# End of a decoder kernel: root table loaded at the down projection, decode tokens over four partition groups, first residual tile ahead of the last tile

## The reference

```python
hp = rms_norm(y_p, g_ffn_pre[l])
hs = rms_norm(y_s, g_ffn_pre[l])
y_p = y_p + rms_norm(swiglu(hp, w_gate[l], w_up[l], w_down[l]), g_ffn_post[l])
y_s = y_s + rms_norm(swiglu(hs, w_gate[l], w_up[l], w_down[l]), g_ffn_post[l])
```

## Time and profile before

| | |
|---|---|
| time before, median of 3 runs | 991.49 us (990.19 to 991.56) |
| the profiled execution | 988.71 us; span from first to last instruction 986.50 |
| granted TensorE clock, mean | 0.985 |
| PE busy | 942.6 us, 96% |
| DVE, ACT, POOL busy | 443.1, 356.3, 170.9 us |
| DMA | 105.85 MB, 107 GB/s over the span |

### The profile page before, as it was taken

One profiled execution on the slowest core, in us unless ns is written; L12 is line 12 of the kernel. 1 busy time (PEld: TensorE's weight loads), 2 busy tenths in 40 slices (PEclk: granted clock), 3 DMA queues, 4 the chain that ended last, 5 costly groups with the idle time before them and its releaser, 6 DMA issues.

```text
span 986.5 us, 18130 instructions
## 1 busy us (share of the span) xinstructions
PE 942.6 (96%) x7734; PEld 876.2 (89%) x7734; DVE 443.1 (45%) x900; ACT 356.3 (36%) x565; POOL 170.9 (17%) x46
## 2 busy tenths in 40 slices
PE   3999999899899999999899999999999999999997
PEld 2999998776699999976379999999999999999996
DVE  5799975765354677111453572222222222001103
ACT  5442224574454463135334543222222222222111
POOL 3000000000000001300030003433333333353330
PEclk9999999889999999999899989999999999999999
DMA  7304205342251358358051101222222232222202
GB/s 213 109 34 130 87 2 199 123 130 87 86 171 54 124 171 295 132 213 341 1 171 44 43 28 60 85 85 85 87 91 94 96 100 75 86 76 75 86 33 91
DMA packets 85343, 105.85 MB, mean 107 GB/s; under 512 B 9473, under 2 KB 72834, under 8 KB 85154
## 3 DMA queue, kind: packets, MB, share of 16 engines
q1 hardware_dynamic: 85056, 104.92, 32.0%
q10 hardware_dynamic: 226, 0.05, 0.0%
HBM read 98.26 MB, written 6.70 MB: 106 GB/s over the span
## 4 chain that ended last, share of the span: by engine, by line
PE 86%; DVE 8%; ACT 3%; issue 2%; DMA 1%; ACTq 0%; DVEq 0%
PE pall L1796 55%; PE pall L1808 7%; PE pall L2130 5%; PE pall L1833 4%; PE pall L2177 2%; PE pall L1820 2%; PE pall L2188 1%; PE pall L1886 1%; PE pall L1986 1%; DVE a_s L1434 1%; PE pall L1869 1%; PE pall L1890 1%; PE pall L2224 1%; PE pall L1995 1%; PE pall L1852 1%
## 5 line engine op out<-in xcount | busy, mean ns | idle before, releaser
L627 POOL TENSOR_TENSOR w_lo<-w_raw,w_hi 128x2048 fp32r<-128x2048 f32 (+1 forms) x36 | 161.2, 4476 | 622.8 <-ACT w_hi L670 332.1
L1796 PE MATMUL pall<-x_hi,w_hi 128*128 128x272 f32 x1024 | 213.5, 290 | 0.0
L1796 PE MATMUL pall<-x_lo,w_hi 128*128 128x272 f32 x1024 | 212.0, 288 | 0.0
L1796 PE MATMUL pall<-x_hi,w_lo 128*128 128x272 f32 x1024 | 210.6, 287 | 0.0
L1796 PEld LDWEIGHTS pall<-x_lo,w_hi 128*128 128x128 f32 x1024 | 161.5, 189 | 0.0
L1796 PEld LDWEIGHTS pall<-x_hi,w_hi 128*128 128x128 f32 x1024 | 160.5, 189 | 0.8
L1796 PEld LDWEIGHTS pall<-x_hi,w_lo 128*128 128x128 f32 x1024 | 160.6, 189 | 0.0
L670 ACT ACTIVATE w_hi<-w_raw 128x2048 fp32r<-128x2048 f32 (+1 forms) x61 | 114.7, 1880 | 91.4 <-PE pall L1796 91.4
L1796 PE MATMUL pall<-g_hi,w_hi 128*128 128x272 f32 x352 | 73.1, 289 | 0.0
L1796 PE MATMUL pall<-g_lo,w_hi 128*128 128x272 f32 x352 | 72.7, 288 | 0.0
L1796 PE MATMUL pall<-g_hi,w_lo 128*128 128x272 f32 x352 | 72.6, 287 | 0.0
(11 more groups left out here) (387 smaller groups left out, 1639.7 us busy)
## 6 DMA issues: line engine op xcount, KB each, us to landing
w_raw<-in_w_gate SPq DMA_DIRECT2D x10, 1024.0 KB, 5.3
w_raw<-in_w_up SPq DMA_DIRECT2D x10, 1024.0 KB, 5.3
w_raw<-in_w_in SPq DMA_DIRECT2D x8, 1024.0 KB, 6.5
w_raw<-in_w_down SPq DMA_DIRECT2D x8, 1024.0 KB, 4.9
dm_kv<-in_cache_mem_v SPq DMA_DIRECT2D x5, 1024.0 KB, 13.9
w_raw<-in_w_out SPq DMA_DIRECT2D x4, 1024.0 KB, 6.1
d_k<-in_cache_k SPq DMA_DIRECT2D x16, 256.0 KB, 3.0
d_v<-in_cache_v SPq DMA_DIRECT2D x16, 256.0 KB, 4.2
```

The costliest lines, as they stand in the source:

```text
L627: e.tensor_tensor(w_lo[:, n % 2, 0:w], w_raw[:, n % 2, 0:w], w_hi[:, n % 2, 0:w].bitcast(F32), ALU.subtract)\
L1796: ins = mm(acc(j)[:, a, :], w, x[:, k_x + k, a * HALF:(a + 1) * HALF], start=first and k == 0 and s_, stop=last and k == kts - 1 and t_)
```

## The change

Five edits, all at the end of the kernel:

1. ACT takes a root that nobody reads before the fourth unit of the down projection (n = `U_DOWN + 3`).
2. The decode tokens' part of `zg` tile k goes to partitions 32(k % 4) to 32(k % 4) + 31, columns 128(k // 4) onwards, of `y_tok[:, 4, :]`, so that the tile is 128 x 256 and not 32 x 1024. The same holds for the decode tile of the residual. Both use a matmul with the identity instead of a transpose. The decode sum is taken four times, once for each group of 32 partitions.
3. One root and one reciprocal of 128 x 5 replace two of each.
4. `y_transposes(0)` moves into `zg_transposes`, between the last two tiles (k = 6 and 7).
5. `y_sample` is stored in four transfers, one for each group of partitions, each row of which holds two pieces of 128 columns.

```diff
+                for q in range(4):
+                    store(O["y_sample"].rearrange("b t (j q c) -> q (b t) j c", j=2, q=4)[q],
+                          y_tok[32 * q:32 * q + 32, t, 0:256].rearrange("p (j c) -> p j c", j=2))
...
+            if n == U_DOWN + 3:
+                e.activation(small[:, 60:61], small[:, EPS_COL:EPS_COL + 1], ACT.Sqrt)
...
-        e.activation(small[:, Y_RSTD:Y_RSTD + 4], bank(4)[:, 0:4], ACT.Sqrt, bias=small[:, EPS_COL:EPS_COL + 1]).then_inc(S("norm_root"), 1)
-        e.activation(small[0:NS_TOK, Y_RSTD + 4:Y_RSTD + 5], bank(4)[0:NS_TOK, 4:5], ACT.Sqrt,
-                     bias=small[0:NS_TOK, EPS_COL:EPS_COL + 1]).then_inc(S("norm_root"), 1)
+        e.activation(small[:, Y_RSTD:Y_RSTD + 5], bank(4)[:, 0:5], ACT.Sqrt, bias=small[:, EPS_COL:EPS_COL + 1]).then_inc(S("norm_root"), 1)
...
-                e.tensor_copy(y_tok[0:NS_TOK, 4, k * P:(k + 1) * P], bank(b + 1)[0:NS_TOK, 0:P]).then_inc(S("zgT_out"), 1)
+                rows = slice(32 * (k % 4), 32 * (k % 4) + 32)
+                e.tensor_copy(y_tok[rows, 4, k // 4 * P:(k // 4 + 1) * P], bank(b + 1)[rows, 0:P]).then_inc(S("zgT_out"), 1)
...
+            cols = D if t < 4 else 256
             e.wait_ge(S("yT_full"), t + 1)
+            e.scalar_tensor_tensor(out=y_tok[:, t, 0:cols], in0=y_tok[:, t, 0:cols], scalar=small[:, Y_RSTD + t:Y_RSTD + t + 1],
+                                   in1=y_banks(t)[:, 0:cols], op0=ALU.mult, op1=ALU.add).then_inc(S("y_ready"), 1)
...
+        def y_transposes(t):
+            for k in range(KT):
+                if t < 4:
+                    ins = e.transpose(y_banks(t)[:, k * P:(k + 1) * P], yT[:, k, t * P:(t + 1) * P], ident[:])
+                else:
+                    rows = slice(32 * (k % 4), 32 * (k % 4) + 32)
+                    ins = mm(y_banks(t)[rows, k // 4 * P:(k // 4 + 1) * P], yT[:, k, NP_TOK:TOK], ident[:], start=True, stop=True)
+            ins.then_inc(S("yT_full"), 1)
...
-                e.transpose(bank(b + 1)[0:NS_TOK, 0:P], zg[:, k % 2, NP_TOK:TOK], ident[:]).then_inc(S("zgT_full"), 1)
+                mm(bank(b + 1)[32 * (k % 4):32 * (k % 4) + 32, 0:P], zg[:, k % 2, NP_TOK:TOK], ident[:], start=True, stop=True).then_inc(S("zgT_full"), 1)
+                if k == KT - 2:
+                    y_transposes(0)
...
-        y_transposes(0)
-
         e.wait_ge(*counted("n5", "add", KT - 1))
         e.wait_ge(S("zgT_out"), 2 * KT - 2)
-        for t in range(5):
-            w = P if t < 4 else NS_TOK
-            ins = mm(bank(4)[0:w, t:t + 1], sqacc[:, t * P:t * P + w], ones[:, 0:1], start=True, stop=True)
+        for t in range(4):
+            mm(bank(4)[:, t:t + 1], sqacc[:, t * P:(t + 1) * P], ones[:, 0:1], start=True, stop=True)
+        for q in range(4):
+            ins = mm(bank(4)[32 * q:32 * q + 32, 4:5], sqacc[:, NP_TOK:TOK], ones[:, 0:1], start=True, stop=True)
         ins.then_inc(S("norm_sum"), 1)
-        e.wait_ge(acc_out, J_DOWN + KT)
         y_transposes(1)
```

More of the change, by code:

```diff
@@ L610, in _ @@
             else:
-                store(O["y_sample"].rearrange("b t d -> (b t) d"), y_tok[0:NS_TOK, t, :])
+                for q in range(4):
+                    store(O["y_sample"].rearrange("b t (j q c) -> q (b t) j c", j=2, q=4)[q],
+                          y_tok[32 * q:32 * q + 32, t, 0:256].rearrange("p (j c) -> p j c", j=2))
         e.wait_ge(S("k_stored0"), 48)
@@ L1760, in _ @@
                 e.tensor_copy(y_tok[:, 0:4, k * P:(k + 1) * P], bank(b).rearrange("p (t c) -> p t c", t=4)).then_inc(S("zgT_out"), 1)
-                e.tensor_copy(y_tok[0:NS_TOK, 4, k * P:(k + 1) * P], bank(b + 1)[0:NS_TOK, 0:P]).then_inc(S("zgT_out"), 1)
-        e.wait_ge(*counted("n5", "root", 2))
-        e.reciprocal(small[:, Y_RSTD:Y_RSTD + 4], small[:, Y_RSTD:Y_RSTD + 4])
-        done(e.reciprocal(small[0:NS_TOK, Y_RSTD + 4:Y_RSTD + 5], small[0:NS_TOK, Y_RSTD + 4:Y_RSTD + 5]))
+                rows = slice(32 * (k % 4), 32 * (k % 4) + 32)
+                e.tensor_copy(y_tok[rows, 4, k // 4 * P:(k // 4 + 1) * P], bank(b + 1)[rows, 0:P]).then_inc(S("zgT_out"), 1)
+        e.wait_ge(*counted("n5", "root", 1))
+        done(e.reciprocal(small[:, Y_RSTD:Y_RSTD + 5], small[:, Y_RSTD:Y_RSTD + 5]))
         e.wait_ge(S("zgT_out"), 2 * KT)
         for t in range(5):
-            rows = P if t < 4 else NS_TOK
+            cols = D if t < 4 else 256
             e.wait_ge(S("yT_full"), t + 1)
-            e.scalar_tensor_tensor(out=y_tok[0:rows, t, :], in0=y_tok[0:rows, t, :], scalar=small[0:rows, Y_RSTD + t:Y_RSTD + t + 1],
-                                   in1=y_banks(t)[0:rows, :], op0=ALU.mult, op1=ALU.add).then_inc(S("y_ready"), 1)
+            e.scalar_tensor_tensor(out=y_tok[:, t, 0:cols], in0=y_tok[:, t, 0:cols], scalar=small[:, Y_RSTD + t:Y_RSTD + t + 1],
+                                   in1=y_banks(t)[:, 0:cols], op0=ALU.mult, op1=ALU.add).then_inc(S("y_ready"), 1)
     @block.tensor
@@ L2324, in _ @@
         zg_transposes(DOWN_C - 1)
-        def y_transposes(t):
-            w = P if t < 4 else NS_TOK
-            for k in range(KT):
-                ins = e.transpose(y_banks(t)[0:w, k * P:(k + 1) * P], yT[:, k, t * P:t * P + w], ident[:])
-            ins.then_inc(S("yT_full"), 1)
-        y_transposes(0)
         e.wait_ge(*counted("n5", "add", KT - 1))
         e.wait_ge(S("zgT_out"), 2 * KT - 2)
-        for t in range(5):
-            w = P if t < 4 else NS_TOK
-            ins = mm(bank(4)[0:w, t:t + 1], sqacc[:, t * P:t * P + w], ones[:, 0:1], start=True, stop=True)
+        for t in range(4):
+            mm(bank(4)[:, t:t + 1], sqacc[:, t * P:(t + 1) * P], ones[:, 0:1], start=True, stop=True)
+        for q in range(4):
+            ins = mm(bank(4)[32 * q:32 * q + 32, 4:5], sqacc[:, NP_TOK:TOK], ones[:, 0:1], start=True, stop=True)
         ins.then_inc(S("norm_sum"), 1)
-        e.wait_ge(acc_out, J_DOWN + KT)
         y_transposes(1)
```

## The result

The changed kernel is slower. Its six runs have a median of 994.32 us (993.43 to 997.08), the kernel before 990.47 (988.68 to 991.56, six runs): ratio 1.0047, 95% interval 1.0034 to 1.0060. Timed again beside the experiments it gave 993.46 against 990.25, ratio 1.0040 (1.0024 to 1.0057). The quotients of the medians alone are 1.0039 and 1.0032. The forecast was 991.9, in a range of 989.2 to 993.2, with a chance of 0.06 for slower by over 0.2%.

The account below looks back on a forecast made before the run. PE was taken to bound the kernel until the last product, store bytes the end after the first residual tile. +0.63 - 0.43 + 0.2 - 0.2 + 0.2 = +0.4 us on 991.49 gave 991.9, range 989.2 to 993.2.

Parts of the forecast that it names:

- the price of the decode part of the zg transposes: Down projection: six added matmul instructions in the PE stream at 0.105 us each, +0.63 us (bounds 0.24 and 0.68).
- The matmuls of tiles 6 and 7: Last two tiles: the seventh and eighth added matmul instructions fall into PE's waits, cost 0.
- The sample stores: End of kernel: four 32 KB stores instead of one of 128 KB, +0.2 us (bounds -0.1 and +0.6).
- the bytes set the end: After the first residual tile, store bytes bind; DVE's last instruction ending 0.86 us earlier is hidden.
- case C: End of kernel: follows DVE's last instruction, not bytes; -0.7 us, or -0.1 at 0.2 per added issue; chance 0.09.
- Case D: End of kernel: the four small stores land late, +2.6 us in all, 994.1; chance 0.06.
- The table load: Root table load moved from the last wait into the down projection: gives back nothing, costs 0, with 3.6 us slack.
- The early tile: Before the last tile's transposes: first residual tile fills PE's idle gap, so the sums start earlier, -0.43 us.
- One root and reciprocal: Norm after the last product: one root and one reciprocal instead of two each, -0.2 us.
- The narrow sums: Norm's sums: the fifth becomes four sums, 8 instructions 32 columns wide, +0.2 us (bounds 0 and 0.88).
- case F: ACT's 1.5 us reach PE, or 16 decode matmuls before the last residual instruction take 1.5 more: +1.9, 993.4; chance 0.03.
- three signs of being wrong: DMA share below 0.9 between fourth prompt and sample stores; last landing over 9 us after first issue; added passes 0.03 us.

Follow-up runs that it names:

- the kernel with full-width transposes: Kernel before with early root and first residual tile, decode tokens transposed full-width onto partitions 96 to 127: ratio 1.0004; with first residual tile stored in halves, 1.0001.
- the early tile alone: Kernel before with only the root taken early and the first residual tile moved between tiles 6 and 7: 990.53 us, ratio 1.0002.

## Why the prediction was wrong

**The step that failed** is the price of the decode part of the zg transposes: "The moving side stays at 128 columns, which makes them like the fillers, so I take 0.105", 6 x 0.105 = +0.63, upper bound 0.68. It measured +2.37, three times 0.78 to 0.80. The number of added instructions, their place in the stream and the 0.11 us of a full-width pass were right. What was missing is the crossing: a plain fp32 matmul with 32 weight columns has its weights loaded only when the full-width matmul ahead is nearly through, and holds up the next full-width load in the same way, shown by the kernels with narrow (1.79), wide (1.24) and side-by-side narrow matmuls (1.31) and by the narrow transposes of before (1.01). The rows taken for the bounds could not show its price: the narrow sums stood side by side, and the fillers were wide. The matmuls of tiles 6 and 7, put at nothing because PE waits there, cost 0.37 us where no early tile stands between them (head 4.95). The trace of before had a row of the right kind, eight transposes followed by narrow matmuls with 256 moving columns (timeline of PE, before):

```profile
434.28 1.04 PE L1833 MATMUL pall<-ident,dm_kv 128*128 128x128 f32 x8
435.25 0.64 PE L2209 MATMUL pall<-dm_kT,dm_qz 128*32 128x256 f32 x8
```

The narrow ones begin 0.97 us behind the start of eight transposes that need 0.88. The Trainium skill (TensorE: Matmul & The Clock Gate, Part 3, The mechanism) says that a weight load overlaps running matmuls only when its group of rows is another one, or into the background buffer. All matmuls in question have weights on all 128 rows, so the rule on rows does not tell them apart here: full-width loads start with the matmul ahead, and so do narrow loads behind narrow matmuls (954.82 behind 954.81). Only the loads at a crossing wait, 0.17 and 0.20 us. Which buffer a load goes to, no run here shows.

**The end of the kernel** is the second step that failed. The sample stores were put at +0.2 (bound +0.6), and the end took 1.06 us longer. The prediction held that after the first residual tile the bytes set the end and hide DVE's shorter last instruction. They did not: a first store 0.53 us earlier won nothing (in the kernel with full-width transposes), and the sample stores began 0.79 us earlier behind the first prompt store, as soon as DVE was done. The order of events is that of case C, which had 0.2 us for an added issue; the four stores went out 0.74 us apart. Case D's mechanism did not occur: the fourth store landed about 2 us after its issue, no later than usual, but it was issued 2.2 us after the first and not 1.4 (0.67 us an issue and the gap, where 0.48 was taken from small loads in a row). The rule of the Trainium skill (DMA: Bandwidth & Descriptors, Rules for kernel authors) against many small transfers pointed the right way; the prediction's estimate of some 3 us by its table was too large. From the first issue of a sample store to the last landing it took 4.13 us instead of 2.29, 1.84 more, since most of each transfer overlaps the next issue (an issue every 0.74 us, a landing after 1.9 to 2.8).

**What held.** The table load gives nothing back and costs nothing (4.4 us of cover left, 3.6 expected). The early tile fills PE's gap: -0.43 expected, -0.36 measured alone (the sums start 0.12 us behind DVE's copy, not 0.05) and -0.49 in the changed kernel. One root and reciprocal: -0.2 expected, 0.69 to 0.52 us. The narrow sums cost less than thought: 8 instructions in four groups take 0.16 us, where eight in one group took 0.33, and the sums together 1.15 us instead of 1.12, +0.03 where +0.2 was taken. The 16 decode matmuls ahead of the last residual instruction load their weights in 0.38 us, not 1.8 (984.05 to 984.43, in four groups side by side), so the second half of case F did not come. Two small terms went unseen: DVE's large copy of tile 6 starts 1.42 us after the last tile's first evacuation (1.30 before), and its small copy 0.12 later behind that. With them the head won 0.22 instead of 0.43.

None of the prediction's three signs of being wrong came, so they did not cover what failed: the DMA share stayed above 1.0 between the fourth prompt store and the sample's, the last landing was 8.1 us behind the first issue, and the added passes were dearer, not cheaper.

**The chances.** The terms left out summed to 2.8 us (3.2 measured by trace, 0.4 forecast), which alone crosses the bound of 2.0 us; the range missed it because the upper bound of the first term was built from rows of another shape. The timed ratios, 1.0047 and 1.0040, are above the 1.0032 that the traces add up to; the second interval contains it, the first (from 1.0034) just does not. Part of the difference lies outside the span that a trace covers: in 3 of 6 and 5 of 11 executions of the changed kernel, and in the one with narrow matmuls side by side, 2.5 to 3.8 us lie around the span, where every other kernel here, before included, has 2.1 to 2.3. By the spans alone the second measurement gives a median of 990.8 against 988.05, a ratio of 1.0028. What the extra time is, no trace shows.

No version here beats the kernel before by a margin that can be timed: the best by its trace, the early tile alone, wins 0.36 us from the last evacuation to the end (4.22 + 1.30 + 7.52 against 4.58 + 1.31 + 7.51), and its ratio is 1.0002.

## What to carry to other kernels

Before spreading a small tile over partition groups, look at what stands around its matmul on PE: here a plain fp32 matmul with 32 weight columns between full-width ones cost 0.39 us more than the transpose that it replaced, 0.11 for its second pass and the rest for two crossings. If it cannot be avoided, it should stand beside other narrow ones. A saving at the end (0.79 us of DVE) is worth only what the stores behind it leave, and cutting a store into four cost more than the saving that it made possible. Price an instruction by a row that has its shape and its neighbours, not by its instruction count.

## What the runs showed of the hardware

A plain fp32 matmul with 32 weight columns between transposes: weight loads stand still for 0.17 us before its own and for 0.20 us before the next full-width one; with 128 weight columns, or as a transpose with 32, neither. Two narrow matmuls in different groups take together the 0.14 us of weight loading that one takes alone. DVE: a 32-partition copy that starts at partition 32, 64 or 96 behind a copy over all 128 starts 0.70 to 0.73 us after it, one on partitions 0 to 31 after 0.60 to 0.61. The next copy over all 128 is late too: for tile 6, where the small copy of tile 5 lay at partition 32 or 96, it starts 0.03 us behind the end of the add ahead of it, and 0.08 to 0.09 us ahead of that end where that small copy lay at partition 0. SP: issuing a 32 KB store takes 0.42 us with one piece a row and 0.67 with two, where a single store of 128 KB took 0.34. The granted clock of attention falls at a different microsecond from execution to execution (197.3 to 200.3 in the traces compared here); sixteen small matmuls there take 2.00 to 3.69 us by it.
